# The raw input's 32 transposes, from TensorE to VectorE blocks and moves inside SBUF

## What is computed

```python
def first_block(x, ...):                       # x: (1, 512, 1024)
    h = rms_norm(x, g_mix)
    z = h @ w_in                               # 3072 columns: u, gb, gc, q, k, v
    y_conv = gb * short_conv(gc * u, conv_w)
    q = rms_norm(q, g_q) * 64 ** -0.5          # per head of 64
    k = rms_norm(k, g_k)
    y_attn = dilated_mixture(q, k, v)
    mix = concat(rms_norm(y_conv, g_conv_out), rms_norm(y_attn, g_attn_out))
    x = x + mix @ w_out                        # the raw x is needed here
    h = rms_norm(x, g_ffn)
    x = x + (silu(h @ w_gate) * (h @ w_up)) @ w_down
...
def s5_mixer(...):                             # second layer
    dt = exp(log_dt)
    abar = exp(a_re * dt) * (cos(a_im * dt), sin(a_im * dt))
```

## Time and profile before

| what | value |
|---|---|
| median of three runs | 996.63 us |
| time of the profiled execution | 998.33 us |
| its span (first to last instruction) | 996.7 us |
| TensorE busy | 975.9 us, 98% |
| VectorE, ScalarE, GpSimd busy | 679.9, 415.0, 171.7 us |
| mean granted TensorE clock | 0.995 |

### The profile page before, as it was taken

How to read it: one execution, slowest core, us unless ns; L and a number is a source line. 1 busy time by engine, 2 the same in 40 slices (tenths; PEclk the granted TensorE clock), 3 DMA queues, 4 the chain that set the end, 5 groups by cost and what they waited for, 6 DMA issues and landing times.

```text
span 996.7 us, 14071 instructions
## 1 busy us (share of the span) xinstructions
PE 975.9 (98%) x4648; PEld 784.3 (79%) x4648; DVE 679.9 (68%) x1218; ACT 415.0 (42%) x671; POOL 171.7 (17%) x298
## 2 busy tenths in 40 slices
PE   6999999999999999999999999999999999989997
PEld 6876777677888888888888876888888887757886
DVE  6585786687676666655346668498978766865656
ACT  5455454634332323333221236945552326652343
POOL 3010101100000000197200000835760000000000
PEclk9999999999999999999999999999999999999999
DMA  6336757232562332334423223332243334542332
GB/s 216 92 92 201 203 165 197 55 97 85 170 188 85 105 104 86 91 109 136 145 90 105 85 75 109 100 85 69 64 106 88 101 100 89 149 116 69 107 89 85
DMA packets 146228, 112.22 MB, mean 113 GB/s; under 512 B 5100, under 2 KB 136428, under 8 KB 146188
## 3 DMA queue, kind: packets, MB, share of 16 engines
q1 hardware_dynamic: 138768, 85.83, 29.3%
q0 software_dynamic: 7184, 25.84, 9.5%
q10 hardware_dynamic: 236, 0.06, 0.0%
HBM read 99.65 MB, written 4.20 MB: 104 GB/s over the span
## 4 chain that ended last, share of the span: by engine, by line
PE 93%; DMA 2%; ACT 2%; DVE 2%; issue 0%; SPq 0%; DVEq 0%
PE bank L623 20%; PE bank L624 19%; PE bank L625 19%; PE bank L884 4%; PE bank L882 4%; PE bank L883 4%; PE bank L657 2%; PE bank L677 2%; PE bank L607 2%; PE bank L608 2%; PE bank L609 2%; PE bank L790 1%; PE bank L792 1%; PE bank L791 1%; PE bank L600 1%; DMA raw<-in_w_a_o_dram 1%
## 5 line engine op out<-in xcount | busy, mean ns | idle before, releaser
L623 PE MATMUL bank<-hH,wH 128*128 128x512 f32 x840 | 329.4, 392 | 0.1
L625 PE MATMUL bank<-hH,wL 128*128 128x512 f32 x840 | 327.0, 389 | 0.0
L624 PE MATMUL bank<-hL,wH 128*128 128x512 f32 x840 | 326.9, 389 | 0.0
L1582 DVE TENSOR_TENSOR wL<-raw,wH 128x1024 fp32r<-128x1024 f32 x155 | 196.3, 1267 | 155.4 <-ACT wH L1133 154.6
L1133 ACT ACTIVATE wH<-raw 128x1024 fp32r<-128x1024 f32 x155 | 164.0, 1058 | 268.1 <-PE bank L625 125.8
L623 PEld LDWEIGHTS bank<-hH,wH 128*128 128x128 f32 x840 | 157.7, 188 | 39.0 <-issue 6.2
L625 PEld LDWEIGHTS bank<-hH,wL 128*128 128x128 f32 x840 | 157.7, 188 | 33.1
L624 PEld LDWEIGHTS bank<-hL,wH 128*128 128x128 f32 x840 | 157.8, 188 | 31.7
L882 PE MATMUL bank<-aH,wH 128*128 (+1 forms) x160 | 62.2, 389 | 0.0
L883 PE MATMUL bank<-aL,wH 128*128 (+1 forms) x160 | 62.2, 389 | 0.0
L884 PE MATMUL bank<-aH,wL 128*128 (+1 forms) x160 | 62.2, 389 | 0.0
(11 more groups left out here) (479 smaller groups left out, 1486.0 us busy)
## 6 DMA issues: line engine op xcount, KB each, us to landing
raw<-in_w_in_dram SPq DMA_DIRECT2D x61, 512.0 KB, 3.7
mraw<-in_w_mod_dram POOLq DMA_DIRECT2D x24, 512.0 KB, 5.1
raw<-in_w_gate_dram SPq DMA_DIRECT2D x22, 512.0 KB, 3.8
raw<-in_w_up_dram SPq DMA_DIRECT2D x22, 512.0 KB, 3.7
raw<-in_w_down_dram SPq DMA_DIRECT2D x22, 512.0 KB, 3.3
raw<-in_w_out_dram SPq DMA_DIRECT2D x16, 512.0 KB, 3.7
pTd<-turned POOLq DMA_DIRECT2D x24, 320.0 KB, 6.3
x_tok<-in_x_dram SPq DMA_DIRECT2D x4, 512.0 KB, 5.5
```

Source lines behind the costliest of these rows:

```text
L623: mm(o, a, hH[:, k, :], start=(k == 0), stop=False)
L624: mm(o, a, hL[:, k, :], start=False, stop=False)
L625: ins = mm(o, b, hH[:, k, :], start=False, stop=(k == KD - 1))
L1582: TT(wL[s.par][:], raw[s.par][:], wH[s.par][:].bitcast(F32), SU).then_inc(lo_done, 1)
```

## The change

The 32 transposes of the raw input leave TensorE, and the copies of their banks leave VectorE. In their place VectorE makes four block transposes, one for each 128 tokens: each turns all 32x32 blocks of a 128x1024 tile in place, into a new buffer `xturn`. Sixteen DMAs on GpSimd's queue then bring the blocks to their partitions in `xT`: each reads 32 partitions and writes 32 partitions, 8 blocks of 128 numbers each, 128 KB. `xT` now holds its tokens in another order until the residual sum, which reads it by a rearranged pattern and writes the result in plain order. `xturn` lies where `L` is written later, so the first `head_max` waits until all sixteen moves have landed (`xmv`). `wo1` becomes two buffers. On ScalarE, `silu_and_sines` moves from behind slot 1's bank to between slot 0's and slot 1's.

```diff
+        xturn = at("xturn", [P, 4, KD, TB, 32], F32, A0 + 90112)
...
+            pool.wait_ge(xtn, TB)
+            for a in range(4):
+                for b in range(4):
+                    pool.dma_start(xT[32 * a:32 * a + 32].rearrange("p k (b n) -> p k b n", b=4)[:, :, b, :],
+                                   xturn[32 * b:32 * b + 32, a].rearrange("p k t j -> p k (t j)")).then_inc(xmv, 16)
...
-            def x_raw(k, bank):
-
-                transposes(bank, [x_tok[:, t, k * P:(k + 1) * P] for t in range(TB)]).then_inc(xt_mm, 1)
...
-                pe.wait_ge(xt_done, KD)
...
             project(Slot(0), each=h1_done)
-            for k in range(3):
-                x_raw(k, PB[2 + k])
...
             project(Slot(1))
-            pe.wait_ge(xt_done, 1)
-            for k in range(3, 6):
-                x_raw(k, (PB[6], PB[7], PB[2])[k - 3])
             project(Slot(2))
-            pe.wait_ge(xt_done, 5)
-            for k in range(6, KD):
-                x_raw(k, PB[k])
...
                     split_hi(sl.next())
-                if between is not None:
-                    between()
+                    if sq is sqq and between is not None:
+                        between()
...
+            def raw_turn(ts):
+
+                for t in ts:
+                    v.transpose(xturn[:, :, :, t, :].rearrange("p a k j -> p k a j"),
+                                x_tok[:, t, :].rearrange("p (k a i) -> p k a i", k=KD, a=4)).then_inc(xtn, 1)
...
+                if first:
+                    dve.wait_ge(xmv, 16 * 16)
                 if last:
                     head_max(i, masks1, lambda: split_lo(gb.next()))
...
-            raw_evac(range(3))
             split_lo(Slot(0, 0).next())
             steps_of_time()
             angles()
-            raw_evac(range(3, 6))
             split_lo(Slot(0, 1).next())
-            raw_evac(range(6, KD))
+            raw_turn(range(TB))
             split_lo(Slot(0, 2).next())
...
-                mark(TT(xT[:, d, :], xT[:, d, :], wo1[:], AD))
+                mark(TT(in_turn(wo1[d % 2]), raw_block(d), in_turn(wo1[d % 2]), AD))
...
-                TT(xT[:, d, :], xT[:, d, :], wo2[d % 2][:], AD).then_inc(x1_rdy, 1)
+                TT(xT[:, d, :], wo1[d % 2][:], wo2[d % 2][:], AD).then_inc(x1_rdy, 1)
```

More of the change, by code:

```diff
@@ L193, in program @@
         nt1, nt2 = at("nt1", [P, S], F32, A0 + 4096), at("nt2", [P, S], F32, A0 + 6144)
-        wo1, wo2 = at("wo1", [P, S], F32, A0 + 8192), tuple(at(f"wo2{j}", [P, S], F32, A0 + 10240 + 4096 * j) for j in range(2))
+        wo1 = tuple(at(f"wo1{j}", [P, S], F32, A0 + 8192 + 4096 * j) for j in range(2))
+        wo2 = tuple(at(f"wo2{j}", [P, S], F32, A0 + 10240 + 4096 * j) for j in range(2))
         tga, tgb = at("tga", [P, KD, S], F32, A0), at("tgb", [P, KD, S], F32, A0 + 16384)
@@ L271, in program @@
         pe_pre, vec_cp, init_v, init_p = (sem(n) for n in ("pe_pre", "vec_cp", "init_v", "init_p"))
-        r0d, xt_mm, xt_done, sqa_rdy, sqd_rdy, tok_ln, tok_rs, tok_nw, xna, xnd, xn_mm, h1h, h1_done, vec_rdy, s5_cv = (
-            sem(n) for n in ("r0d", "xt_mm", "xt_done", "sqa_rdy", "sqd_rdy", "tok_ln", "tok_rs", "tok_nw", "xna", "xnd",
+        r0d, xtn, xmv, sqa_rdy, sqd_rdy, tok_ln, tok_rs, tok_nw, xna, xnd, xn_mm, h1h, h1_done, vec_rdy, s5_cv = (
+            sem(n) for n in ("r0d", "xtn", "xmv", "sqa_rdy", "sqd_rdy", "tok_ln", "tok_rs", "tok_nw", "xna", "xnd",
                              "xn_mm", "h1h", "h1_done", "vec_rdy", "s5_cv"))
@@ L1648, in _, with raw_block, in_turn @@
             split_lo(Slot(1))
[L1650 to L1655, removed]
+            def raw_turn(ts):
+                for t in ts:
+                    v.transpose(xturn[:, :, :, t, :].rearrange("p a k j -> p k a j"),
+                                x_tok[:, t, :].rearrange("p (k a i) -> p k a i", k=KD, a=4)).then_inc(xtn, 1)
+            def raw_block(d):
+                return xT[:, d, :].rearrange("p (b t j) -> p t b j", b=4, t=TB)
+            def in_turn(t):
+                return t[:].rearrange("p (t b j) -> p t b j", b=4, t=TB)
             def par(k):
@@ L1859, in _ @@
                     dve.wait_ge(wk_mm, d + 1)
-                mark(TT(wo1[:], oc[:], rc[:], MU))
+                mark(TT(wo1[d % 2][:], oc[:], rc[:], MU))
                 TT(wo2[d % 2][:], oa[:], ra[:], MU).then_inc(gfree[sl.par], 1)
```

## The result

The changed kernel takes 1000.01 us in the median of twelve runs (997.63 to 1004.43), and the kernel before, on the same chips, 996.17 us (twelve runs, 994.32 to 998.15). The ratio is 1.0048, with a 95% interval of 1.0037 to 1.0060: slower by about half a per cent, 4.8 us by the ratio and 3.8 us between the medians. The twelve runs are not spread evenly: eight lie between 997.63 and 1000.64, four between 1003.70 and 1004.43.

A forecast was written before the change was run, and what follows sets the result against it. TensorE, busy 975.9 of 996.7 us, was taken as the bound. With the clock falling, -0.3 + 2.5 = +2.2 us on the median 996.63 gave 998.8 us, the moves adding nothing; range 995.3 to 1003.5.

The forecast's parts named there:

- First term: Ahead of head_sums: 3.2 of the 3.49 us removed become a TensorE wait for ScalarE's late sines and copy; -0.3 us.
- the variant in which all 3.49 us come back: Ahead of head_sums: ScalarE is not late at all, the full saving is kept, 993.1 us; chance 0.03.
- Second term: Behind TensorE's wait at head_sums: the granted clock falls, somewhat more likely than not; +2.5 us if so.
- Third term: At the first head_max: the sixteen moves land at 58.0; +1.8 us if TensorE is in time, nothing if the clock fell.
- The transposes' 1.24 us each: VectorE's four block transposes before slot 4: 4.95 us in all, hidden with 0.2 us to spare.
- The residual sum's rearranged reads: In VectorE's residual sum: reads in pieces of 32 numbers, 0.687 us each before, counted as costing nothing.
- clock stays, moves late: At the first head_max: full clock, but TensorE slips behind the moves; +1.8 us, 998.4 us; chance 0.26.
- very late: Before the first head_max: last move lands at 64.4, +8.2 us, a clock fall adds 2.5; 1005 to 1007; chance 0.13.
- the prediction's estimate: Moves by the 8-of-16-ports rule, 189 GB/s: 11.1 us, last landing near 60, TensorE slips by nearly 4 us.

The follow-up runs named there:

- sines_back: Changed kernel with ScalarE's sines moved back behind slot 1's bank; 994.85 us, ratio 0.9991 to the kernel before.
- sines_only: Kernel before, all transposes kept, with only the sines moved between slot 0's and slot 1's banks; 996.91 us, ratio 1.0001 to the kernel before.
- both_back: Changed kernel with sines back behind slot 1's bank and xturn in mixH's place; 994.93 us, ratio 0.9977 to the kernel before.
- own_place: Changed kernel with xturn over mixH instead of L, so head_max waits for no move; 997.23 us, ratio 1.0017 to the kernel before.
- sums_free: both_back, with head_sums no longer waiting for ScalarE's copy of slot 2's bank; 993.63 us, ratio 0.9970 to the kernel before.
- mraw_later: Changed kernel with GpSimd holding the loads of w_mod_2 until the moves have landed; 999.93 us, ratio 1.0037 to the kernel before.
- wide_moves: Changed kernel with four moves, each from 32 partitions to all 128, instead of sixteen; 1007.76 us, ratio 1.0106 to the kernel before.
- filled: Changed kernel with three unused float32 matmuls in TensorE's wait ahead of head_sums; 1003.13 us, ratio 1.0082 to the kernel before.
- place_filled: Changed kernel with xturn in mixH's place and three unused matmuls ahead of head_sums; 998.74 us, ratio 1.0024 to the kernel before.
- after_again: The changed kernel measured again, nothing altered; 1001.11 us, ratio 1.0054 to the kernel before.

## Why the prediction was right, and where its terms were off

The forecast was 998.8 us and most likely within half a per cent; it is 1000.0 and a ratio of 1.0048, just inside that bound, with an interval that reaches 1.0060. As a change it was too small: +2.2 us forecast, +4.8 measured, and clear of noise, which I had not expected of anything under 5 us. The sum up to slot 6 was +2.2 us and measured +2.35 in the first profile, but two of its terms were off and made up for each other, which is luck. The other course makes up most of the difference.

- **First term, -0.3 us** (the waiting sines take back the transposes' time): -3.49 + 3.18 = -0.31. Right, with its mechanism: released by ScalarE's copy to `vT`, ScalarE idle 5.84 us for the angles. `sines_back` and `sines_only` show that it takes both halves of the change. What I had wrong is the copy's share. I called half of the last transposes' time (0.87 us) its cover; with ScalarE in time, the copy alone makes TensorE wait 1.05 us (`both_back`), so the variant in which all 3.49 us come back was not open to this order.
- **Second term, +2.5 us if the clock falls:** the mechanism is shown, the size was too large for this wait. It measured 1.5 us (the rest column), and 1.62 alone in `own_place`; at the second wait, in the other course, it is 2.5 (1.52 and 1.01). I had priced it from sixteen products and "somewhat more in the next ones" in the earlier trace rows. The same place in other traces shows how far that price itself moves, and that the fall does not always come: the same wait and the same sixteen products take 4.53 us before, 3.80 in the changed kernel and 2.37 with the sines alone, where the clock stayed.

```profile
898.02 3.80 PE L684 MATMUL bank<-pT,vt2n 128*64 128x512 f32 x16 [2.79 <-DVE szb L2270]
...
896.20 2.37 PE L677 MATMUL bank<-pT,vt2n 128*64 128x512 f32 x16 [2.79 <-DVE szb L2271]
```

  The first row is of the changed kernel, the second of `sines_only`. The clock stayed there in three of the twelve profiles (`sines_only`, `sums_free`, `mraw_later`) and fell in nine. So the one row that I took the fall from was itself one outcome of two.

- **Third term, nothing if the clock fell:** it was 1.17 us. I took `head_max` to be ready at 58.4 and the moves at 58.0. The moves were in at 58.05, as forecast; but TensorE came 1.7 us earlier, 1.0 of it by the cheaper clock and 0.5 by its earlier start of slot 0. That the moves met their 58.0 is partly luck: they began at 42.05 and not at 43.0, and took 16.0 us and not 15.0. An issue takes 0.58 us, so the queue is done sooner than I had it, but the engines are slower: the weights beside the moves are 1.55 MB at 65 engine-us per MB (`mraw_later`) and not 1.05 MB at 52, and the moves 75 and not 71.
- **The transposes' 1.24 us each:** 4.62 for four, 1.21 us as the mean of one. Slot 4 did not wait. The residual sum's rearranged reads take 0.682 us each, before 0.687. Right.
- **The rival "clock stays, moves late", +1.8 us:** this was the step that failed. By their times, four of the twelve runs go this way, and it costs 7.0 us, not 1.8. I let TensorE slip by the moves' lateness alone (58.0 against 56.2). In the profile the last move landed 43.56 us behind slot 0, where `head_max` had started at 39.11 before, so it was 4.45 us late; TensorE, 0.3 us early, waited 4.75 us; the clock fell within that wait, and 2.5 us came on top, 1.52 ahead of slot 6 and 1.01 behind it. I had given a fall at that place alone only to the "very late" case. That case, at 1005 to 1007, is close to the four runs at 1004, though the moves were not that late.
- **Partitions and ports.** The moves of `mraw_later` and `wide_moves` read 32 partitions and write 32 or all 128, and both need 17 us, with weights beside them. By the rule of the Trainium skill's page "SBUF — State Buffer", section "Door 1: The DMA port swizzle", the last move would have landed near 60, the prediction's estimate. That is 43.0 us behind slot 0; the two profiles of the changed kernel have 41.5 and 43.6, which neither shows nor contradicts the rule, and no run here shows the moves without weights beside them, which would decide it.

What stays open: which course an execution takes when TensorE's wait is 3.2 us. The wait is the same to 0.03 us, and the clock fell in three profiles (changed, own place, loads after the moves) and stayed in two (changed again, four moves). Also open is about 0.9 us: the ratio says +4.8 us (3.7 to 6.0), and eight runs at +2.4 with four at +7.0, counted up to slot 9, make 3.9, which is inside the interval. `filled` measured +8.2 (6.5 to 9.8) where its trace accounts for 6.6, and `place_filled` +2.4 (1.5 to 3.3) where its trace accounts for 1.5. The wait near 892 us adds scatter to every kernel here, the one before included.

## What to carry to other kernels

Work that is taken off the bounding engine may also have covered others: before pricing a removal, list what the other engines did during it. Here 3.49 us of transposes covered a copy (1.05 us) and could have covered late sines (3.2 us), so removing them pays only when the order on ScalarE and the waits on TensorE are changed with it. And when a buffer is borrowed, ask who waits for its return on which engine, and what is queued behind that wait.

## What the runs showed of the hardware

- A TensorE idle time of 3.2 us sometimes brings the granted clock to 0.50 and sometimes does not, in the same kernel: in the two profiles of the changed kernel once each, with its variants in three profiles and not in two. The wait of 2.79 us near 892 us brought it in nine of the twelve profiles and not in three. Of the other waits behind slot 0, those of 0.99 to 1.69 us and one of 2.26 us (`mraw_later`) did not, and those of 2.60 and 2.99 us (`wide_moves`), 4.50 (`filled`) and 4.75 us (`after_again`) did, each of these in a single profile.
- A fall at the first wait cost 1.5 to 1.6 us of this stream, one at the second wait 2.3 and 2.5 us, of which 0.9 and 1.0 us lie behind slot 6.
- A block transpose of 128x1024 float32 numbers took 1.21 us when it read runs of 32 numbers, and 1.98 us when it read every fourth.
- Moving 2.1 MB inside SBUF in pieces of 512 bytes took 75 engine-us per MB (`mraw_later`), more than the weights from memory beside it (65), and 16 to 18 us in all with weights beside it, whether issued as 16 DMAs or as 4.
